# A mixture-of-experts trunk on one core: router and last LayerNorm rearranged, merged activations by token tile, gate products issued ahead of up products

## What is computed

```python
q, k, v, g, u_lru, gate_lru, gate_logits = jnp.split(x @ w_in, splits, axis=-1)
...
merged = gate_ret * (ret @ w_ret_o) + gate_rec * (lru @ w_lru_o)
x = _layer_norm(DEEPNORM_ALPHA * x + merged @ w_out, ln1_g, ln1_b)
moe = _hier_moe(x, w_group, b_group, w_exp_router, b_exp_router, w_e_gate, w_e_up, w_e_down)
return _layer_norm(DEEPNORM_ALPHA * x + moe, ln2_g, ln2_b)
```

## Time and profile before

| | |
|---|---|
| median of 3 runs | 1273.75 us (1272.39 to 1274.04) |
| the profiled execution | 1270.7 us |
| its span, first to last instruction | 1269.0 us |
| mean granted TensorE clock | 0.996 |
| PE busy | 1235.6 us (97%) |
| DVE, ACT, POOL busy | 656.9, 422.3, 60.9 us |
| read from memory | 284.91 MB |

### The profile page before, as it was taken

How to read it: one execution, slowest core, us unless ns; L and a number is a source line. 1 busy time by engine, 2 the same in 40 slices (tenths; PEclk the granted TensorE clock), 3 DMA queues, 4 the chain that set the end, 5 groups by cost and what they waited for, 6 DMA issues and landing times.

```text
span 1269.0 us, 16140 instructions
## 1 busy us (share of the span) xinstructions
PE 1235.6 (97%) x6100; PEld 832.1 (66%) x6100; DVE 656.9 (52%) x934; ACT 422.3 (33%) x600; POOL 60.9 (5%) x68
## 2 busy tenths in 40 slices
PE   7999999999999999999999999999999999998897
PEld 6888888888888888888888888333343343333332
DVE  5587765336365356347334845344454444444445
ACT  4778773223342333333343411311111111111114
POOL 0000000000000000000015100100000000000000
PEclk9999999999999999999999999999999999999999
DMA  7333322363223223223223399999999999999993
GB/s 235 108 86 96 101 66 86 95 176 93 90 67 103 86 72 100 86 66 99 83 68 99 112 407 423 361 413 404 417 418 409 416 413 415 413 418 417 413 423 163
DMA packets 143368, 286.02 MB, mean 225 GB/s; under 512 B 11733, under 2 KB 109125, under 8 KB 118736
## 3 DMA queue, kind: packets, MB, share of 16 engines
q1 hardware_dynamic: 139616, 276.81, 58.5%
q0 software_dynamic: 2544, 4.25, 1.0%
q10 hardware_dynamic: 1152, 4.19, 0.9%
HBM read 284.91 MB, written 4.33 MB: 228 GB/s over the span
## 4 chain that ended last, share of the span: by engine, by line
PE 87%; DMA 11%; DVE 1%; ACT 0%; SPq 0%; issue 0%; DVEq 0%; ACTq 0%
PE bank L1443 19%; PE bank L1445 19%; PE bank L1444 19%; PE bank L1735 14%; DMA m_raw<-in_w_e_up_dram 11%; PE bank L1765 6%; PE bank L1789 4%; PE bank L1725 1%; PE bank L1505 1%; PE bank L1758 1%; PE bank L1829 1%; PE bank L1574 1%; PE bank L1649 0%; DMA vec_rows<-in_b_merge_dram 0%; PE bank L1496 0%; PE bank L1498 0%
## 5 line engine op out<-in xcount | busy, mean ns | idle before, releaser
L1735 PE MATMUL bank<-m_raw,xe 128*64 128x512 f32 x1024 | 233.4, 598 | 13.8 <-DMA m_raw<-in_w_e_up_dram 13.0
L882 DVE TENSOR_TENSOR w_lo<-raw,w_hi 128x1024 fp32r<-128x1024 f32 x120 | 148.2, 1238 | 175.8 <-ACT w_hi L561 174.7
L1443 PE MATMUL bank<-xt_hi,w_hi 128*128 128x512 f32 x576 | 225.3, 391 | 0.5 <-DVE w_lo L882 0.5
L1445 PE MATMUL bank<-xt_hi,w_lo 128*128 128x512 f32 x576 | 224.2, 389 | 0.0
L1444 PE MATMUL bank<-xt_lo,w_hi 128*128 128x512 f32 x576 | 224.1, 389 | 0.0
L878 DVE TENSOR_TENSOR x<-x,bank 128x1024 f32<-128x1024 f32 x120 | 141.2, 1218 | 100.6 <-PE bank L1789 99.7
L561 ACT ACTIVATE w_hi<-raw 128x1024 fp32r<-128x1024 f32 x120 | 125.9, 1056 | 161.8 <-PE bank L1445 159.5
L1735 PEld LDWEIGHTS bank<-m_raw,xe 128*64 128x64 f32 x1024 | 71.8, 136 | 135.4 <-issue 133.0
L1443 PEld LDWEIGHTS bank<-xt_hi,w_hi 128*128 128x128 f32 x576 | 108.1, 188 | 24.1 <-issue 1.5
L1445 PEld LDWEIGHTS bank<-xt_hi,w_lo 128*128 128x128 f32 x576 | 108.1, 188 | 22.7
L1444 PEld LDWEIGHTS bank<-xt_lo,w_hi 128*128 128x128 f32 x576 | 108.2, 188 | 22.0
(11 more groups left out here) (280 smaller groups left out, 1663.4 us busy)
## 6 DMA issues: line engine op xcount, KB each, us to landing
m_raw<-in_w_e_gate_dram SPq DMA_DIRECT2D x64, 1024.0 KB, 27.6
m_raw<-in_w_e_up_dram SPq DMA_DIRECT2D x64, 1024.0 KB, 26.7
m_raw<-in_w_e_down_dram SPq DMA_DIRECT2D x64, 1024.0 KB, 27.6
raw<-in_w_in_dram SPq DMA_DIRECT2D x88, 512.0 KB, 3.8
raw<-in_w_ret_o_dram SPq DMA_DIRECT2D x16, 512.0 KB, 3.4
raw<-in_w_lru_o_dram SPq DMA_DIRECT2D x16, 384.0 KB, 3.3
raw<-in_w_out_dram SPq DMA_DIRECT2D x8, 512.0 KB, 3.7
x_rows<-in_x_dram ACTq DMA_DIRECT2D x4, 512.0 KB, 5.6
```

The costliest lines, as they stand in the source:

```text
L882: return dve.tensor_tensor(dst, a, b_r.bitcast(F32), ALU.subtract)
L1443: pe.matmul(dst, sh, mh, start=first and x == 0, stop=False)
L1445: ins = pe.matmul(dst, sl, mh, start=False, stop=last and x == n - 1)
L1735: last = pe.matmul(bank[side:side + ROWS, 0, :], xe[:, 4 * half + k, :], w[:, FE * k:FE * k + FE], start=half == 0 and k == 0, stop=half = ...
```

## The change

- **Merged activations by token tile.** `mrg_hi` and `mrg_lo` become two buffers `mrg[0]` and `mrg[1]`, for tiles 0, 1 and 2, 3, each laid out by tile, high and low part, k. Each copy and each subtraction is done once for each buffer. The buffers' places and the order of the slots in `m_raw` change with it, and so do the waits of the first 21 loads: loads 0 and 1 wait for nothing more, load 2 for the whole merge, load 6 for the last split of `w_out`, loads 13 to 16 for one tile of the projection each. The residual x comes in four loads, two of them ahead of the LayerNorm's vectors.
- **Router.** The 36 router columns become the stationary operand and the turned tile streams 128 columns. The logits come out turned, ACT adds the bias on the way to `logit_t` (three tiles at once, then the last), PE turns them back by four transposes into PSUM, and DVE reads them there; its own addition is gone.
- **The last tile's LayerNorm by halves.** `mid` is made half by half for every tile, and `x2_ok` is counted after each half of the last. `turn_x2(3)` waits for each half; three identity products stand ahead of it and four in its middle, the two behind it go. ACT's `x2t_out(t - 1)` stands ahead of the square root of tile t.
- **Lists, picks and expert 0.** Four small DVE operations on the weights move behind `hot_r`; `sel`, the copy to `rows_0` and the copy to `xe` go by halves; 20 of the 32 list records move behind the turns of the picked rows.
- **Gate products ahead of up.** `gate_up` waits for the gate load, makes its four products, waits for the up load, and makes its four.

```diff
-        mrg_hi, mrg_lo = at("mrg_hi", 160, [P, KD, TOKENS], F32R), at("mrg_lo", 176, [P, KD, TOKENS], F32R)
+        mrg = [at("mrg_01", 160, [P, 2, 2, KD, P], F32R), at("mrg_23", 80, [P, 2, 2, KD, P], F32R)]
...
-        m_raw = [at(f"m_raw{n}", kb, [P, 2048]) for n, kb in enumerate((80, 88, 96, 104, 112, 120, 40, 48, 56, 0, 8, 144, 152, 160, 168, 176, 184, 16, 24, 32, 192))]
+        m_raw = [at(f"m_raw{n}", kb, [P, 2048]) for n, kb in enumerate((112, 120, 96, 104, 176, 184, 40, 48, 56, 0, 8, 144, 152, 160, 168, 80, 88, 16, 24, 32, 192))]
...
-        logit = rt("logit", TT * 36)
         w_rt = rt("w_rt", KD * 36)
-        b_rt = rt("b_rt", 36)
+        b_rt = rt("b_rt", 1)
+        logit_t = at("logit_t", 138, [P, TOKENS])
...
-            sp.wait_ge(split_done, U_END + RING)
-            sp.wait_ge(units_done, U_OUT + RING)
+            def load_x2(t):
+                sp.wait_ge(units_done, U_RET3 + t + 1 + RING)
+                sp.dma_start(x2[:, t, :], x_view[t]).then_inc(res_in, 16)
+
+            for t in (0, 1):
+                load_x2(t)
+            sp.wait_ge(split_done, U_OUT + 6 + RING)
             sp.dma_start(ln1[:, 0, :], row(io["ln1_g"])).then_inc(ln1_in, 16)
             sp.wait_ge(qk_split, 4 * HEADS)
             sp.dma_start(ln1_b_in[:, :], row(io["ln1_b"])).then_inc(ln1_in, 16)
-            sp.dma_start(x2[:, :, :], io["x"][0].rearrange("(t p) d -> p t d", p=P)).then_inc(res_in, 16)
-
-
-            sp.wait_ge(mrg_split, KD)
+            for t in (2, 3):
+                load_x2(t)
 
             def load_m(n, src):
+                if n == 2:
+                    sp.wait_ge(mrg_split, KD)
+                if n == 6:
+                    sp.wait_ge(split_done, U_END + RING)
                 if n == 9:
                     sp.wait_ge(proj_ok, TT)
-                if n == 13:
-                    sp.wait_ge(proj_ok, 2 * TT)
+                if 13 <= n < 17:
+                    sp.wait_ge(proj_ok, TT + n - 12)
                 if n == 19:
-                    sp.wait_ge(x2_ok, TT)
+                    sp.wait_ge(x2_ok, TT + 1)
...
-                    copy(mrg_hi[:, k, :], acc[:, k, :]).then_inc(mrg_hi_ok, 1)
+                    act.wait_ge(acc_ok, KD)
+                    for side in range(2):
+                        last = copy(mrg[side][:, :, 0, k, :], acc[:, k, 256 * side:256 * side + 256].rearrange("p (t n) -> p t n", t=2))
+                    last.then_inc(mrg_hi_ok, 1)
...
+                if t:
+                    x2t_out(t - 1)
                 act.wait_ge(x2_var, t + 1)
                 act.activation(scale_v[:, 0:1], mv[:, 1:2], ACT.Sqrt).then_inc(x2_std, 1)
-                if t:
-                    x2t_out(t - 1)
             x2t_out(TT - 1)
+            act.wait_ge(router_in, 96)
+            for n, cols in ((TT - 1, slice(0, P * (TT - 1))), (TT, slice(P * (TT - 1), TOKENS))):
+                act.wait_ge(routed, n)
+                act.activation(logit_t[0:36, cols], bank[0:36, 6 + n // TT, cols], ACT.Identity, bias=b_rt[0:36, 0:1]).then_inc(biased, 1)
...
-            copy(rows_0[:, :], bank[:, 4, :]).then_inc(rows_ok, 1)
+            for half in range(2):
+                copy(rows_0[:, 256 * half:256 * half + 256], bank[:, 4, 256 * half:256 * half + 256]).then_inc(rows_ok, 1)
             act.wait_ge(xe_turned, 1)
-            copy(xe[:, :, :].rearrange("p (h k) n -> p k h n", h=2), bank[:, 5, :].rearrange("p (k h n) -> p k h n", h=2, n=ROWS)).then_inc(xe_ok, 1)
+            for half, ok in enumerate((xe_ok, xe_rest)):
+                copy(xe[:, 4 * half:4 * half + 4, :], bank[:, 5, :].rearrange("p (k h n) -> p h k n", h=2, n=ROWS)[:, half, :, :]).then_inc(ok, 1)
...
-                    sub(mrg_lo[:, k, :], acc[:, k, :], mrg_hi[:, k, :]).then_inc(mrg_split, 1)
-
-
-            dve.wait_ge(res_in, 16)
+                    for side in range(2):
+                        last = sub(mrg[side][:, :, 1, k, :], acc[:, k, 256 * side:256 * side + 256].rearrange("p (t n) -> p t n", t=2), mrg[side][:, :, 0, k, :])
+                    last.then_inc(mrg_split, 1)
...
-                step(dve.scalar_tensor_tensor(mid, z, mv[:, 0:1], g, ALU.subtract, ALU.mult))
-                dve.wait_ge(std, t + 1)
-                step(dve.reciprocal(scale_v[:, 1:2], scale_v[:, 0:1]))
-                step.wait()
                 for c_ in range(2):
                     cols = slice(512 * c_, 512 * c_ + 512)
+                    step(dve.scalar_tensor_tensor(mid[:, c_, :], z[:, c_, :], mv[:, 0:1], g[:, c_, :], ALU.subtract, ALU.mult))
+                    if c_ == 0:
+                        dve.wait_ge(std, t + 1)
+                        step(dve.reciprocal(scale_v[:, 1:2], scale_v[:, 0:1]))
+                    step.wait()
                     last = dve.scalar_tensor_tensor(end(x2[:, t, cols]), start(mid[:, c_, :]), scale_v[:, 1:2], end(ln[:, 1, cols]), ALU.mult, ALU.add)
+                    if c_ == 0 and t == TT - 1:
+                        last.then_inc(ok, 1)
...
-            dve.wait_ge(routed, TT)
-            lg = logit[:, :].rearrange("p (t n) -> p t n", t=TT)
-            step(tt(lg, bank[:, 6, 0:TT * 36].rearrange("p (t n) -> p t n", t=TT),
-                    b_rt[:, :].unsqueeze(1).to_broadcast([P, TT, 36]), ALU.add))
-            step.wait()
+            dve.wait_ge(routed, TT + 1)
+            lg = bank[:, 4, 0:TT * 36].rearrange("p (t n) -> p t n", t=TT)
...
-            dve.wait_ge(exp_ok, 2)
-            step(dve.tensor_reduce(red[:, :], exps.rearrange("p (t n) -> p t n", t=TT), AX, ALU.add))
-            step.wait()
-            step(dve.scalar_tensor_tensor(red[:, :], diff, 1.0, red[:, :], ALU.add, ALU.mult))
-            step.wait()
-            step(dve.reciprocal(wts[:, 0:TT], red[:, :]))
-            step.wait()
-            step(tt(wts[:, TT:2 * TT], wts[:, 0:TT], diff, ALU.mult))
...
-            tt(sel[:, :, :], iota_t[:, 1:ROWS + 1].unsqueeze(1).to_broadcast([P, TT, ROWS]),
-               place.unsqueeze(2).to_broadcast([P, TT, ROWS]), ALU.is_equal).then_inc(sel_ok, 1)
+            for half in (slice(0, 2), slice(2, TT)):
+                tt(sel[:, half, :], iota_t[:, 1:ROWS + 1].unsqueeze(1).to_broadcast([P, 2, ROWS]),
+                   place[:, half].unsqueeze(2).to_broadcast([P, 2, ROWS]), ALU.is_equal).then_inc(sel_ok, 1)
...
             def turn_x2(t):
-                pe.wait_ge(x2_ok, t + 1)
+                if t < TT - 1:
+                    pe.wait_ge(x2_ok, t + 1)
                 if t:
                     pe.wait_ge(x2t_ok, t)
                 for k in range(KD):
+                    if t == TT - 1 and k == 0:
+                        pe.wait_ge(x2_ok, TT)
+                    if t == TT - 1 and k == 4:
+                        keep_warm(4)
+                        pe.wait_ge(x2_ok, TT + 1)
                     last = pe.transpose(bank[:, 4 + k // 4, P * (k % 4):P * (k % 4) + P], x2[:, t, P * k:P * k + P], ident[:, :])
...
-                    last = pe.matmul(bank[:, 6, 36 * t:36 * t + 36], x2_t[:, t % 2, P * k:P * k + P], w_rt[:, 36 * k:36 * k + 36],
+                    last = pe.matmul(bank[0:36, 6 + t // (TT - 1), P * t:P * t + P], w_rt[:, 36 * k:36 * k + 36], x2_t[:, t % 2, P * k:P * k + P],
...
+            def turn_logits(t):
+                return pe.transpose(bank[:, 4, 36 * t:36 * t + 36], logit_t[0:36, P * t:P * t + P], ident[0:36, 0:36])
 
             router(1)
             router(2)
+            keep_warm(3)
             turn_x2(3)
-            keep_warm(2)
             router(3)
+            pe.wait_ge(biased, 1)
+            for t in range(TT - 1):
+                turn_logits(t)
+            pe.wait_ge(biased, 2)
+            turn_logits(TT - 1).then_inc(routed, 1)
...
-            pe.wait_ge(sel_ok, 1)
             for t in range(TT):
+                pe.wait_ge(sel_ok, 1 + t // 2)
...
+            lists_part(range(3))
             for k in range(NEAR):
+                pe.wait_ge(rows_ok, 1 + k // 2)
                 last = pe.transpose(bank[:, 5, P * k:P * k + P], rows_0[:, P * k:P * k + P], ident[:, :])
             last.then_inc(xe_turned, 1)
+            lists_part(range(3, 2 * TT)).then_inc(first_built, 1)
...
+            def gate_up_part(half, side, w):
+
+                for k in range(4):
+                    last = pe.matmul(bank[side:side + ROWS, 0, :], xe[:, 4 * half + k, :], w[:, FE * k:FE * k + FE],
+                                     start=half == 0 and k == 0, stop=half == 1 and k == 3)
+                last.then_inc(m_done, 1)
+
             def gate_up_half(half, gate, up):
 
-                for k in range(4):
-                    for side, w in ((0, gate), (ROWS, up)):
-                        last = pe.matmul(bank[side:side + ROWS, 0, :], xe[:, 4 * half + k, :], w[:, FE * k:FE * k + FE],
-                                         start=half == 0 and k == 0, stop=half == 1 and k == 3)
-                        if k == 3:
-                            last.then_inc(m_done, 1)
```

(51 more changed lines are left out.)

9 lines of the change are left out of this document (5 added, 4 removed).

## The result

The changed kernel takes **1366.5 us** (median of 4, 1365.97 to 1367.98) against 1273.07 for the kernel before, measured beside it (1271.59 to 1274.04): a ratio of 1.074, 95% interval 1.072 to 1.076. The forecast was no change, 1272.9 in a range up to 1290.

What follows compares the result with a forecast made beforehand. The weight stream, restarted by expert 0's first gate product, was taken to bound the kernel, with little PE slack. Merge +0.4 and gate start -1.25 gave -0.85: 1269.85 profiled, 1272.9 against the median, range 1269.8 to 1290.

Steps and rivals of the forecast that it cites:

- What bounds the kernel: From 799 us on, the weight stream, its end moving with the first gate product; PE's slack against it 13.0 us.
- Gate products ahead of up: Expert loop: four gate then four up products keep the rate; cost 0, bounds 0 and 3.1 us per half.
- The rival of a limited distance: Expert loop: each step the up side starts late costs 16 us first (1289), 29 each further; chance 0.06.
- One side blocks the other: Expert loop: waiting records hold back the other side's later ones, +3.1 us per half, kernel 1461; chance 0.16.
- Merged activations, +0.4: Split copies and subtractions delay the seventh operand pair, stalling PE near 731 by 0.4 us, bounds 0 and 2.4.
- The last LayerNorm, -1.1: Last router ends near 778.9 instead of 780.03: the 0.85 wait for ACT's copy goes and full clock returns.
- The turned logits and the 26 products: Between router and ranks: DVE is 0.9 us earlier, but the 26 warm-up products start only 0.5 earlier.
- Behind the picks: Copy, turn and copy before expert 0's gate, done by halves with list products moved: 0.4 us less.
- The clock falls again: Front: clock stays at 0.50 during warm-up products and turns, costing 2.5 us more, kernel 1274.5; chance 0.12.
- the front's gain arrives whole: Third rival: no merge stall, warm-up products not limiting; -2.6 to -3.2 us, about 1271.0; chance 0.18.
- moved up by 3.05: Whole kernel: the sum, made against the profiled 1270.7 us, is raised by 3.05 to compare with the median 1273.75.
- What would show it: Signs: half and expert times, DMA share well below 1 if blocked, gate near 792.0, hole before first release over 5 us.

Runs made afterwards that it cites:

- a: The rest alone without the seven warm-up products at the last turn and with 22 for 26 behind the logits: 1268.41 us, ratio to before 0.9972.
- c: The rest alone with fewer warm-up products and with merged activations, slots and first loads as before: 1268.82 us, ratio to before 0.9965.
- the router run: The kernel before with only the router part changed (router columns stationary, 128 columns streamed): 1270.05 us against 1272.82, ratio 0.9981.
- (b): The rest alone with merged activations, slots and first loads as in the kernel before: 1270.20 us, ratio to before 0.997.
- the rest alone: The changed kernel with gate and up products alternating again: 1270.71 us against 1273.33, ratio 0.998; run once more, 1270.26, ratio 0.9976.

## Why the prediction was wrong, point by point

- *What bounds the kernel*: right. PE had 13.0 us of slack and an expert's PE time set the rest as soon as that was used; with the alternating order the end follows the first gate product (above, a and c).
- **The step that failed is "Gate products ahead of up: I take 0, the value nearest to what rows 5 show".** Rows 5 show that one waiting record is passed over; from this I took seven. The true reach is three. The term is four steps, 1.77 us per half (5.42 against 3.65), between the bounds 0 and 3.1 that I gave. Over the kernel it is +109.7, less 13.0: +96.7.
- *The rival of a limited distance* named the mechanism: its own arithmetic gives 1289 + 3 x 29 = 1376 for four steps, against 1366.5; with steps of 0.43, the distance at which records start, instead of 0.45 (3.65 / 8, with the longer first step and the tail) it is 1370, and the clock of the front, 2.8 us in the router run, accounts for most of the remainder of 3.5. Two choices were wrong: its chance of 0.06, and that the range was closed at one step. Between "one record is passed over" and "seven are" no row spoke for seven, so this case and the full block deserved most of the chance.
- *One side blocks the other* (1461) is refuted: with three waiting the up record runs. The Trainium skill, TensorE: Matmul & The Clock Gate, Part 3, says that matmuls start and end in program order. The runs disagree on both: at 907.39 a record starts ahead of three that precede it in the program, and with 643 ns it is over at 908.03, before the sixth gate record (started at 907.81, 592 ns); the starts are measured, the ends are modelled by the profile. The same section gives PE a "64-deep reorder window", by which it pulls weight loads ahead of matmuls in flight. How far one column side passes the other it does not say; here it was three waiting records.
- *Merged activations, +0.4*: 0.39 at the seventh pair (731.12 to 731.74 for a pitch of 0.23). By the end of the projection it is 0.75 in this trace (770.83 - 9.20 against 769.53 - 8.65) and 0.5 between (b) and the rest alone, so more than the stall itself arrived; where the rest comes from is not seen.
- *The last LayerNorm, -1.1*: the last router ended 9.43 behind the start of the last projection product (770.83 to 780.26), forecast 9.37 (769.53 to 778.9). Right, the clock included, though (a) shows that the warm-up products were not needed for it.
- *The turned logits and the 26 products*: their start came 0.27 earlier instead of 0.5 (10.06 against 10.33 from the last projection product), since the turns take 0.70 with their wait. So the picks came 0.42 earlier, not 0.8. *Behind the picks*, 0.44 for a forecast of 0.4. In all -0.86 for -1.25; with the merge's +0.75 for +0.4 the first gate product came 0.11 earlier where the sum had 0.85. (The sign "near 792.0" left out the merge's 0.4; the sum itself has it. The gate stood at 793.64, and at 793.04 in the rest alone.)
- *The clock falls again* and *the front's gain arrives whole*: neither. 1.00 throughout, and also in (a) with fewer warm-up products. The rest alone is 2.6 below before, the number of the third rival, but not by its mechanism: its gate moved by 0.16.
- **A second step failed without showing in the total**: "moved up by 3.05" from the profiled execution to the median. Those 3.05 go with the lower clock of the typical run, and the change removes most of that: the rest alone has its profiled execution (1270.78) at its median (1270.71). For the rest alone my sum would have said 1272.9; it is 1270.7 and 1270.3.
- *What would show it*: "6.7 and about 20 if one side blocks, 3.65 and 13.88 if right" was the right place to look; the answer lay between them, 5.42 and 17.41. The DMA share was the wrong sign: it stayed at 0.98 while the stream lost a tenth of its rate. From 794 to 799 the rate fell from 128 to 61 GB/s, as the longer hole was to show.

## What to carry to other kernels

Where two column tiles of TensorE are to run at once, write their products alternating, or at most two products (four records) of one side at a time: a record of the other side started only once no more than three stood unstarted ahead of it, whatever their length. A block of n records (6, 8 and 16 were run) ahead of the other side costs n - 4 steps of one record. Within that reach a separate wait for each side's weights might be had for nothing; no run here tried it.
When the trace shows that a queue reorders, it does not show how far; a change that leans on a longer distance needs a range that holds every distance in between.
And when a profiled execution is 0.2% below the median, look at the granted clock of the other runs before the difference is carried over unchanged.

## What the runs showed of the hardware

- A float32 product of 512 columns on a 64-column side is two records at a pitch of 0.43 us (905.62 on), one of 256 columns two at 0.216: cut in half and alternated they take 3.73 instead of 3.65 for a half, with twice the weight loads, which the slack covered here (1270.87 in one run, waits for weights 9.5 us instead of 13.0).
- The reach of TensorE's queue over the other column side is three waiting records: the up side started with record 1 of 4, 3 of 6, 5 of 8 and 13 of 16.
- With router products of 36 columns and a PE wait of 0.85 to 0.88 us behind them, the granted clock fell to 0.50 there in six traces of seven, for 3.4 or 6.8 us; with router products of 128 columns it stayed at 1.00 in seven traces of seven, a PE wait of 0.70 in one of them included. The router part alone lowered the median by 2.8 us (ratio 0.9981, 0.9965 to 0.9997).
